# Gelu by tanh in some expert slots, three tiles merged as one group, and work moved into the lead-in

## The reference

```python
def layer(x, cond, lw, rope, ctx_cache):
    sh1, sc1, g1, sh2, sc2, g2 = jnp.split(jax.nn.silu(cond) @ lw['w_mod'] + lw['b_mod'], 6, axis=-1)
    h = rmsnorm(x, lw['g_attn_norm']) * (1 + sc1) + sh1
    mix, new_ctx = branches(h, lw, rope, ctx_cache)
    x = x + g1 * mix
    h = rmsnorm(x, lw['g_ffn_norm']) * (1 + sc2) + sh2
    x = x + g2 * peer(h, lw['w_pq'], lw['peer_keys'], lw['peer_u'], lw['peer_v'])
    return x, new_ctx

def peer(h, w_pq, keys, u_tab, v_tab):
...
        q = (hb @ w_pq).reshape(t, P_HEADS, 2, P_QDIM // 2)
        sc = jnp.einsum('thpd,hpkd->thpk', q, keys).astype(jnp.float32)
        sv, si = lax.top_k(sc, P_TOPK)
...
        cv, ci = lax.top_k(cand, P_TOPK)
        eidx = jnp.take_along_axis(cidx, ci, axis=-1)
        gate = jax.nn.softmax(cv, axis=-1)
        act = jax.nn.gelu(jnp.einsum('thkd,td->thk', u_tab[eidx], hb).astype(jnp.float32))
        return jnp.einsum('thk,thkd->td', (gate * act).astype(hb.dtype), v_tab[eidx])
```

## Time and profile before

| | |
|---|---|
| time, median of 3 runs | 5408.85 us (5403.55 to 5409.71) |
| the profiled execution's own time | 5399.06 us |
| its span, first to last instruction | 5397.2 us |
| PE, DVE, ACT, POOL busy | 4051.1 (75%), 2902.5 (54%), 1901.2 (35%), 1562.8 (29%) us |
| bytes moved by DMA | 1736.05 MB, mean 322 GB/s |
| table loads on ACT before Gelu (L1182) and before Exp (L1137) | 116 and 107, 1283 ns each |

### The profile page before, as it was taken

How to read it: one execution, slowest core, us unless ns; L and a number is a source line. 1 busy time by engine, 2 the same in 40 slices (tenths; PEclk the granted TensorE clock), 3 DMA queues, 4 the chain that set the end, 5 groups by cost and what they waited for, 6 DMA issues and landing times.

```text
span 5397.2 us, 64023 instructions
## 1 busy us (share of the span) xinstructions
PE 4051.1 (75%) x20878; PEld 1700.6 (32%) x20878; DVE 2902.5 (54%) x6321; ACT 1901.2 (35%) x5143; POOL 1562.8 (29%) x1453
## 2 busy tenths in 40 slices
PE   5849877786779976567876897777686897656666
PEld 3434444332233332122222344443323333211111
DVE  2175633246584587644458554332737547884544
ACT  0113277522232333225323225771223333333333
POOL 0004411112233333333333342111133333343332
PEclk8879988898879987787887898889797998876666
DMA  8536644587999999999999664349699999899998
GB/s 309 207 133 234 229 135 139 220 341 300 394 403 400 391 375 391 420 382 381 401 416 398 230 233 149 132 149 366 243 421 383 396 407 379 330 420 420 420 420 368
DMA packets 247577, 1736.05 MB, mean 322 GB/s; under 512 B 28368, under 2 KB 30416, under 8 KB 42448
## 3 DMA queue, kind: packets, MB, share of 16 engines
q0 software_dynamic: 184320, 1342.26, 63.2%
q1 hardware_dynamic: 62928, 389.70, 18.3%
HBM read 1726.47 MB, written 5.37 MB: 321 GB/s over the span
## 4 chain that ended last, share of the span: by engine, by line
PE 36%; DMA 25%; DVE 22%; ACT 8%; issue 6%; DVEq 2%; POOL 1%; ACTq 1%; SPq 1%; POOLq 0%
DMA arena<-in_experts,arena 20%; PE ps L1050 10%; PE ps L817 10%; DVE sq L1519 7%; DMA arena<-in_weights 4%; PE ps L955 3%; PE ps L1003 3%; PE ps L1028 2%; PE ps L1016 2%; PE ps L980 1%; ACT L1182 1%; DVE arena L1251 1%; ACT arena L1137 1%; DVE arena L1249 1%; DVE arena L1254 1%
## 5 line engine op out<-in xcount | busy, mean ns | idle before, releaser
L790 POOL DMA_INDIRECT arena<-in_experts,arena x1280 | 1408.5, 1100 | 3378.0 <-PE ps L1050 3100.7
L1050 PE MATMUL ps<-arena 64*64 64x512 f32 x10240 | 1730.4, 754 | 821.3 <-ACT arena L1188 808.1
L1519 DVE CUSTOM_DVE_ANT_0 sq<-arena 128x1024 f32<-128x1024 f32 x1280 | 1569.0, 1226 | 884.3 <-DMA arena<-in_experts,arena 779.4
L1182 ACT ACTIVATE arena<-arena 128x1 f32<-128x1 f32 x1280 | 257.6, 201 | 2078.3 <-DVE arena L1519 2076.4
L1050 PEld LDWEIGHTS ps<-arena 64*64 64x64 f32 x10240 | 330.7, 152 | 1822.4 <-issue 1798.5
L817 PE MATMUL ps<-arena 128*128 128x512 f32 (+3 forms) x1920 | 833.5, 575 | 57.6 <-DMA arena<-in_weights 57.5
L1188 ACT ACTIVATE arena<-ident,arena 128x128 f32<-128x128 f32 x1280 | 515.1, 402 | 93.0 <-issue 5.4
L817 PEld LDWEIGHTS ps<-arena 128*128 128x128 f32 x1920 | 351.1, 194 | 539.6 <-issue 502.8
L1184 ACT ACTIVATE arena<-arena 128x1 f32<-128x1 f32 x1280 | 376.8, 294 | 91.6 <-issue 4.5
L1028 PE MATMUL ps<-arena 128*128 128x128 f32 (+1 forms) x2048 | 375.4, 336 | 7.2 <-issue 7.2
L1028 PEld LDWEIGHTS ps<-arena 128*128 128x128 f32 x2048 | 309.8, 214 | 185.1 <-issue 169.9
(11 more groups left out here) (161 smaller groups left out, 3033.8 us busy)
## 6 DMA issues: line engine op xcount, KB each, us to landing
arena<-in_weights SPq DMA_DIRECT2D x316, 1024.0 KB, 8.9
arena<-in_experts,arena POOLq DMA_INDIRECT x1280, 12.6
arena<-mod_rows SPq DMA_DIRECT2D x24, 512.0 KB, 7.0
arena<-in_weights SPq DMA_DIRECT2D x16, 576.0 KB, 8.0
arena<-in_weights SPq DMA_DIRECT2D x8, 768.0 KB, 6.1
arena<-in_weights SPq DMA_DIRECT2D x12, 512.0 KB, 4.9
arena<-in_x_sample SPq DMA_DIRECT2D x8, 512.0 KB, 15.5
arena<-in_g_norm SPq DMA_DIRECT2D x8, 512.0 KB, 11.8
```

What stands on the lines that cost most here:

```text
L790: nc.gpsimd.indirect_dma_start(out=ring[BUF[n]], out_offset=None, in_=ins["experts"], in_offset=bass.IndirectOffsetOnAxis(ap=index(t)[:, s ...
L1050: last = MM(acc[h][to:to + 64, :], diag[n % 4][lo:lo + 64, lo:lo + 64], ring[BUF[n]][lo:lo + 64, D + c * 512:D + (c + 1) * 512], start=s = ...
L1182: A(gel[:, c:c + 1], dots[:, c:c + 1], ACT.Gelu_apprx_tanh)
L1519: V.tensor_tensor_reduce(out=sq[:], in0=ring[BUF[n]][:, 0:D], in1=h2_of_slot(n), scale=1.0, scalar=0.0, op0=ALU.mult, op1=ALU.add, accum_o ...
```

## The change

- `GROUPS`: tiles 2, 3 and 4 are one group. Its merge and routing lie over slots -2 to 124 of the 512, in both layers; the second choices of tiles 3 and 4 over 140 to 220 and 260 to 340. Ring buffers 6 and 7 are freed by the group's last `pq`, buffer 8 by its last `o`. Buffers for merged tiles, queries and scores are laid out for three tiles.
- `by_tanh`: in the slots of tile 0 of both layers and of tiles 2 to 4 of layer 0, gelu is made from Square, Copy with the gate as scale, Identity, Tanh and Identity, with half the gate (`tkg` multiplies by 0.5). In the other slots it stays Gelu and Copy.
- Lead-in: the first norms of the latent tiles go between the prompt's inputs, the modulation of layer 1 between the prompt's heads, and the latents' `u`, `qc` and `cq` products between the prompt's routing (`mixed`). `sample(0)` no longer has them.
- In layer 0 the constants and the prompt of layer 1 lie over slots 130 to 440.
- The modulation of each layer has its own semaphores; every product waits for its tile's transposed norm; the first latent head's Exp of layer 0 waits for the stored modulation of layer 1, since the modulation's rows lie in its scratch.

```diff
-GROUPS = {0: (0,), 1: (1,), 2: (2,), 3: (3, 4)}
+GROUPS = {0: (0,), 1: (1,), 2: (2, 3, 4)}
...
+def by_tanh(l, t):
+
+    return t == 0 or (l == 0 and t >= 2)
...
+EARLY = ("u", "qc", "cq")
+
+
+def mixed(items, more):
+
+    per, given, s = len(more) / len(items), 0, []
+    for i, it in enumerate(items):
+        s.append(it)
+        n = int(per * (i + 1) + 1e-6)
+        s += more[given:n]
+        given = n
+    return s + more[given:]
...
 def prompt(l):
 
-    norms = first_norms(l, (0,))
+    norms, inputs, heads = first_norms(l, (0,)), inputs_of(l, (0,)), attention(l, (0,))
+    routed = route(l, 0, 0)
     if l == 0:
...
-    s = norms + inputs_of(l, (0,)) + attention(l, (0,))
-    s += [("rows2", l, 0), ("keys", l, 0)] + merge(l, 0) + route(l, 0, 0)
-    return s
+        inputs = mixed(inputs, first_norms(0, SAMPLE))
+        heads = mixed(heads, mod_items(1))
+        routed = mixed(routed, [i for i in inputs_of(0, SAMPLE) if i[0] in EARLY])
+    return norms + inputs + heads + [("rows2", l, 0), ("keys", l, 0)] + merge(l, 0) + routed
...
-    s = first_norms(l, SAMPLE) + inputs_of(l, SAMPLE) + attention(l, SAMPLE)
+    s = first_norms(l, SAMPLE) + inputs_of(l, SAMPLE) if l else [i for i in inputs_of(l, SAMPLE) if i[0] not in EARLY]
+    s += attention(l, SAMPLE)
...
-        line.spread(-2, 96, pieces(merge(l, 2) + route(l, 2, 2)))
-        line.spread(96, 236, pieces(merge(l, 3) + route(l, 3, 3)))
-        line.spread(240, 300, choose(l, 4))
+        line.spread(-2, 124, pieces(merge(l, 2) + route(l, 2, 2)))
+        line.spread(140, 220, choose(l, 3))
+        line.spread(260, 340, choose(l, 4))
         if l == 0:
-            line.spread(238, 320, [("consts", 1)] + mod_items(1))
-            line.spread(320, 500, pieces(prompt(1)))
+            line.spread(130, 440, pieces([("consts", 1)] + prompt(1)))
...
-           6: lambda l: ("pq", l, 2, 15), 7: lambda l: ("pq", l, 3, 15), 8: lambda l: ("tk1", l, 3, 15, 1)}
+           6: lambda l: ("pq", l, 2, 15), 7: lambda l: ("pq", l, 2, 15), 8: lambda l: ("o", l, NT - 1, 1)}
...
                     act.wait_ge(dot_done, n + 1)
-                    A(gel[:, c:c + 1], dots[:, c:c + 1], ACT.Gelu_apprx_tanh)
-                    act.drain()
-                    A(wts[:, c:c + 1], gel[:, c:c + 1], ACT.Copy, scale=gate(n // SLOTS % NT)[:, s:s + 1])
+                    if by_tanh(*ETILES[e]):
+                        A(of(cube), of(dots), ACT.Square, scale=GELU_B ** 0.5)
+                        A(of(share), of(dots), ACT.Copy, scale=gate(e % NT)[:, s:s + 1])
+                        act.drain()
+                        A(of(inner), of(cube), ACT.Identity, scale=of(dots), bias=of(dots))
+                        act.drain()
+                        A(of(gel), of(inner), ACT.Tanh, scale=GELU_A)
+                        act.drain()
+                        A(of(wts), of(gel), ACT.Identity, scale=of(share), bias=of(share))
+                    else:
+                        A(of(gel), of(dots), ACT.Gelu_apprx_tanh)
+                        act.drain()
+                        A(of(wts), of(gel), ACT.Copy, scale=gate(e % NT)[:, s:s + 1])
```

More of the change, by code:

```diff
@@ L576, in build @@
         merged = lambda t: pm(6144, D) if t == 0 else pm(6144 + D * GROUPS[GROUP_OF[t]].index(t), D)
-        sg = lambda j, t: pm((7168, 8192)[side(t)] + 512 * (j % 2), 512)
-        pqb = lambda gid, q: pm(7168 + P * (q % 2), P) if gid == 0 else pm(9216 + 256 * (q % 2), 256)
-        scb = lambda gid, q: pm(7424 + P * (q % 2), P) if gid == 0 else pm(9728 + 256 * (q % 2), 256)
+        sg = lambda j, t: pm((7168, 9216)[side(t)] + 512 * (j % 2), 512)
+        pqb = lambda gid, q: pm(7168 + P * (q % 2), P) if gid == 0 else pm(6144 + 384 * (q % 2), 384)
+        scb = lambda gid, q: pm(7424 + P * (q % 2), P) if gid == 0 else pm(6912 + 384 * (q % 2), 384)
         g2 = ar(C0 + D + 4 * P, D)
@@ L605, in build @@
         esum = take(8)
-        dots, gel, wts = (take(16) for _ in range(3))
+        dots, gel, wts, cube, inner, share = (take(16) for _ in range(6))
         assert _e[0] <= C0 + D
@@ L631, in build @@
         w_land = [semaphore(f"w_land{b}") for b in range(NU)]
-        bmod_in, mod_stored = semaphore("bmod_in"), [semaphore(f"mod_stored{b}") for b in range(2)]
+        bmod_in, mod_stored = semaphore("bmod_in"), [[semaphore(f"mod{l}_stored{b}") for b in range(2)] for l in range(L)]
         rows1_in, rows2_in, g2_in = semaphore("rows1_in"), semaphore("rows2_in"), semaphore("g2_in")
@@ L694, in _ @@
                         dst = modd[l][:, a * D:b * D].rearrange("p (n g j) -> p n g j", g=4, j=P)[:, :, g, :]
-                        sp.dma_start(dst, arena[32 * g:32 * g + 2, MOD0[l] + 256 * a:MOD0[l] + 256 * b].rearrange("p (n j) -> p n j", j=P)).then_inc(mod_stored[half], 16)
+                        sp.dma_start(dst, arena[32 * g:32 * g + 2, MOD0[l] + 256 * a:MOD0[l] + 256 * b].rearrange("p (n j) -> p n j", j=P)).then_inc(mod_stored[l][half], 16)
                 elif kind == "rows1":
                     c = item[2]
-                    sp.wait_ge(mod_stored[0], 64 * (l + 1))
+                    sp.wait_ge(mod_stored[l][0], 64)
                     if l and c == 0:
                         sp.wait_ge(*ready("n2", l - 1, NT - 1))
-                        sp.wait_ge(*ready("tk1", l - 1, LAST_GROUP, 15, 1))
+                        sp.wait_ge(*ready("tk1", l - 1, LAST_GROUP, 15, 2))
                     elif l:
@@ L708, in _ @@
                     c = item[2]
-                    sp.wait_ge(mod_stored[1], 64 * (l + 1))
+                    sp.wait_ge(mod_stored[l][1], 64)
                     sp.wait_ge(*ready("om", l, (0, NT - 1)[c], 1))
@@ L788, in _ @@
                         before = RELEASE[BUF[n]](l)
-                        pool.wait_ge(*(full if before[0] in ("pq", "sw") else ready)(*before))
+                        pool.wait_ge(*(full if before[0] in ("pq", "sw", "o") else ready)(*before))
                     nc.gpsimd.indirect_dma_start(
@@ L863, in _ @@
                     t = item[2]
[L864 to L865 removed]
+                    pe.wait_ge(*ready("hT1", l, t))
                     cols = {"kv": 288, "cq": QL, "kc": 256}.get(kind, 512)
@@ L1090, in _ @@
                     k0, half = item[2:]
-                    if k0 == 0 and l:
-                        act.wait_ge(mod_stored[1], 64 * (l + 1))
                     if half == 0:
@@ L1106, in _ @@
                     if item[2] == 1:
-                        act.wait_ge(mod_stored[1], 64 * (l + 1))
+                        act.wait_ge(mod_stored[l][1], 64)
                     out(A(zt(item[2])[:, 0:512], src, ACT.Gelu_apprx_tanh))
@@ L1132, in _ @@
                     n = len(unit_tiles(t, m)) * P + m
+                    if (t, m, h) == (1, 0, 0) and l == 0:
+                        act.wait_ge(mod_stored[1][1], 64)
                     act.wait_ge(max_ready, j)
@@ L1513, in _ @@
                     dve.drain()
-                    done(TT(g3, g3, esum.unsqueeze(2).to_broadcast([P, H, TOPK]), ALU.mult))
+                    done(STT(g3, g3, 0.5 if by_tanh(l, t) else 1.0, esum.unsqueeze(2).to_broadcast([P, H, TOPK]), ALU.mult, ALU.mult))
                     dve.drain()
```

8 lines of the change are left out of this document (3 added, 5 removed).

## The result

The changed kernel takes 5438.33 us (median of 4, 5429.69 to 5443.87), the kernel before beside it 5406.33: a ratio of 1.0057, interval 1.0040 to 1.0075. It is slower by 0.6% where 2.1% faster was forecast, and lies above the range. The profiled execution took 5429.69 us, its span 5427.9 against 5397.2: **+31 us where the sum said -117**.

The account below looks back on a forecast made before the run. DMA was taken to bound tiles 1 to 4, TensorE's products and the latent heads tile 0. Terms 72 - 158 - 18 - 63 + 50 = -117 gave 5399 - 117 + 10 = 5292 us, range 5195 to 5420.

Parts of the forecast that it names:

- The failed step: Layer 0's tile 0: TensorE 0.92 busy in products, -117 us; 0.90 in heads, -46; layer 1's heads likewise, -63.
- The heads gain little: Rival, tile 0's heads: hand-overs from TensorE to VectorE to ScalarE keep TensorE's idle time; taken as 5398 us; chance 12 in 100.
- ScalarE did not bind layer 0's last tiles: Rival, layer 0's slots 124 to 512: ScalarE binds, 388 slots take 1377 us, not 1145; 5524 us; chance 10 in 100.
- no loads stayed: Rival, both heads stretches: Square or Tanh doesn't share Exp's set, table loads stay; 5519 us; chance 5 in 100.
- the merged stretch was not free: Rival, slots to 124: they keep before's pace and DMA's saving is collected; 5010 us; chance 5 in 100.
- A switch that holds ScalarE beyond its load: Rival, heads: each table switch also costs a drain, so heads fall to 254 and 246 us; 5175 us; chance 4 in 100.
- Lead-in, +87 for +72: Before layer 0's first slot: norms +13, modulation +32, early products and first slot's wait; 459 us instead of 387, +72.
- Their six loads have room: Lead-in, prompt's routing: the early products' six weight loads fit beside DMA traffic of 169 GB/s.
- The rest of tile 0, +15 for +5: Layer 0's tile 0 behind the heads: the rest gets 5 more slots, +5 us.
- layer 1's products and rest, +9 for 0: Layer 1's tile 0 outside the heads: the longer ScalarE chain costs nothing there, 0 us.
- The longer chain beside products costs nothing while TensorE leads at 7 us per slot: Layer 1's tile 0: ScalarE's chain of 2.25 us for 1.05 adds no time beside products.
- The merge of three tiles: Tiles 1 to 4, both layers: 558 us to slot 124, then 1145 and 993; in all -18 and +50 us.

## Why the prediction was wrong, by its steps

**The failed step: the busy share that was taken for TensorE in tile 0, 0.92 in the products and 0.90 in the heads, where 0.74 and 0.81 were measured.** The work was right: 162 us left in the products (159 measured), 254 and 246 us at full speed in the heads (282 x 0.89 = 251 and 270 x 0.90 = 243 measured). With the measured shares in their place the same working gives 162 / 0.74 = 219, 254 / (0.81 x 0.89) = 352 and 246 / (0.81 x 0.90) = 337, against 216, 348 and 334 measured. This is 105 of the 148 us between forecast and result: 59 in the products, 24 and 22 in the heads. The 0.92 stood in no row; TensorE was busy 0.89 there before, and with the cover in place. The 0.90 was said to lie between the heads' 0.79 and that 0.89, but it lies above both.

For the products the reason is shown. The moved products were what TensorE did during the norms' hand-overs: taking them out raised its idle time from 29 to 57 us, and the stretch without slots is idle for 37 too. I named the cover for other edits but did not ask what these products themselves covered. That 159 meets 162 is partly luck: the forecast's cut held 19 us of the heads, and the clock that was granted fell. In the table's cut its sum is 251 - 84 - 16 = 151, at 0.92 a stretch of 165 us. Of the 59 us, some 44 are then idle time, and some 8 each come of the lower clock (0.87 for 0.95) and of the cut.

For the heads the reason is shown in part. I had the chain's instructions in ScalarE's sum, 213 us where 207 was measured (213 counted 49 slots, and 57 stood there), and held the sum against the stretch, as if what fits beside TensorE cost nothing. Cutting the chain takes off 28 and 21 us, about what was missing (24 and 22), but that the sizes meet is luck: 17 and 12 of them are TensorE's busy time at a higher clock. Idle time fell from 67 to 56 us in layer 0, where a share of 0.90 would have left 31. What holds the rest is open.

**Rivals.** "The heads gain little" was the nearest: it named the hand-overs, but left the heads none or a third of the gain and looked only there; with tanh alone seven tenths of the two gains came (39 and 40 of 46 and 63), in the changed kernel six tenths (22 and 41). ScalarE did not bind layer 0's last tiles (1124 us at DMA share 0.98, ScalarE busy 0.63), no loads stayed, the merged stretch was not free. A switch that holds ScalarE beyond its load is what the Trainium skill has on its page "ScalarE: Activation LUTs", section "What ACT_TABLE_LOAD costs". By that rule, as the prediction priced it, the two heads would have come to 254 and 246 us; with tanh alone they took 331 and 335. Hand-overs alone could keep them there, so the rows decide. ScalarE was idle for 0.8 us in all before the 44 loads of Exp and for 0.8 before those of Gelu, and Exp starts 0.01 us after its load.

**Lead-in, +87 for +72.** The merge ended at 334 us, as worked out, and the early products took the 76 us that were reckoned:

```profile
L838 PE MATMUL ps<-arena 128*128 128x512 f32 x128 | 56.0, 593 | 1.8 <-DMA arena<-in_weights 1.8
L1048 PE MATMUL ps<-arena 128*128 128x128 f32 x256 | 38.0, 312 | 16.4 <-DMA arena<-in_weights 15.3 <-issue 1.2
L838 PE MATMUL ps<-arena 128*128 128x384 f32 x64 | 21.2, 487 | 0.0
```

These are TensorE's groups from 334 to 477 us: 56.0 + 21.2 = 77. What was missed are 17 us of waits for weights (15.3 and 1.8), most of them before the query products of the routing. "Their six loads have room" was true of DMA's share (0.33) and still not enough, since a load is issued in SP's order, behind TensorE's use of the ring's buffer. What SP waited for from 320 to 480 us:

```profile
SPq L684 <- PE ps L1048: 91.5, 8, 21.0
SPq L684 <- PE ps L838: 48.9, 6, 17.3
```

**The rest of tile 0, +15 for +5, layer 1's products and rest, +9 for 0.** "The longer chain beside products costs nothing while TensorE leads at 7 us per slot" was wrong by 6 to 9 us per stretch with tanh alone; the version with tanh in the heads alone gets 4 to 15 us back in each. Of the 15 slots that left the products 8 came to the heads, as worked out, and 7 to the rest, where 5 were counted.

**Right.** The merge of three tiles: 577 and 583 us to slot 124 where 558 was forecast, then 1124 and 981 for 1145 and 993. So was its reason: TensorE sets the merge, busy 304 of the first 315 us, and DMA, at 287 and 277 GB/s to slot 124, can't collect the bytes that were saved. The 19 and 25 us over the forecast lie in the routing behind the merge (262 us in layer 0, forecast 243). VectorE's work was to set it; VectorE is busy 0.73 there and TensorE 0.71, and TensorE waits 66 us for the slots' diagonals. The merge turned the result: alone it costs 97 us, three times the whole loss. The forecast held it together with the modulation that left layer 0's tiles, and set it against a gain in tile 0 that came only in part.

## What to carry to other kernels

Before work is moved out of a stretch, ask what it covered there: take the waits of the stretch without it for the bound, not its busy share with it. Where engines hand a unit on in turn, an instruction can cost part of its time on any of them, however low their busy shares: here 48 us less on ScalarE (207 to 159) made a stretch 28 us shorter. Merging saves bytes only where DMA ends last in the stretch that holds the merge; here it made a stretch that TensorE binds, and the bytes were not collected.

## What the runs showed beyond that

The distance between a slot and its last product weighs more than any part of the change: 0.4 slots less cost 127 us and one slot more 313 (5565 and 5751 against 5438). An instruction on 128x1 elements takes 0.15 to 0.16 us on VectorE and 0.19 to 0.39 on ScalarE, where each operand from memory adds some 0.1 (Tanh 0.20, Copy with a scale 0.28, Identity with scale and bias 0.39). And the granted clock carried much of what layer 0's heads gained: 0.85 before, 0.90 with tanh alone, 0.94 with the cut chain, while TensorE's busy share went from 0.78 to 0.81 and 0.83. That the shorter gaps raised the clock is not shown: in the version with tanh in the heads alone both layers' heads are busy 0.80, at a clock of 0.88 and 0.92.
